# Seven-product multiplication kept for the second MLP matrix only, with weight sums moved from GpSimd to accumulating transfers and VectorE

## The reference

```python
    hf = rmsnorm(x, g_pre_ff)
    ff = jnp.einsum('btf,fd->btd', jnp.square(jax.nn.relu(jnp.einsum('btd,df->btf', hf, w_ff1) + b_ff1)), w_ff2) + b_ff2
    x = x + rmsnorm(ff, g_post_ff)
```

## Time and profile before

| what | us |
|---|---|
| median of 3 runs | 1292.96 (1291.39 to 1293.85) |
| time of the profiled execution | 1292.42 |
| its span, first to last instruction | 1290.9 |
| TensorE busy | 1203.9 |
| VectorE busy | 938.9 |
| ScalarE busy | 578.5 |
| GpSimd busy | 335.7 |

### The profile page before, as it was taken

The page is one execution under the profiler, slowest core; times in us unless marked ns, Lnnn a source line. Parts: engine busy times, 40 slices in busy tenths (PEclk is TensorE's granted clock), DMA queues, the critical chain, the costliest instruction groups (busy, mean ns, idle before and its releaser), DMA issues.

```text
span 1290.9 us, 23168 instructions
## 1 busy us (share of the span) xinstructions
PE 1203.9 (93%) x8749; PEld 1130.1 (88%) x8749; DVE 938.9 (73%) x1287; ACT 578.5 (45%) x914; POOL 335.7 (26%) x303
## 2 busy tenths in 40 slices
PE   9999999999999999999999999992898798799784
PEld 9999888978978888899999999992898798799783
DVE  6833888888888888874554333476778888888886
ACT  6433533543453453355432223564555544544543
POOL 4010011001101101100000000067557656656642
PEclk9999999999999999999999999995999899899888
DMA  6352244516516525422222234231232233232221
GB/s 215 108 178 100 66 160 169 170 57 226 182 43 233 189 65 175 152 94 87 87 92 83 80 97 151 83 152 35 64 115 67 75 93 95 66 98 83 66 103 69
DMA packets 47755, 145.97 MB, mean 113 GB/s; under 512 B 4756, under 2 KB 7188, under 8 KB 47304
## 3 DMA queue, kind: packets, MB, share of 16 engines
q1 hardware_dynamic: 36120, 103.74, 25.2%
q0 software_dynamic: 11424, 41.23, 9.1%
q10 hardware_dynamic: 144, 0.09, 0.0%
HBM read 120.54 MB, written 24.49 MB: 112 GB/s over the span
## 4 chain that ended last, share of the span: by engine, by line
PE 79%; DVE 12%; POOL 3%; issue 3%; ACT 3%; DMA 0%; DVEq 0%; ACTq 0%; POOLq 0%
PE product L2094 63%; PE side L2094 16%; POOL xg L746 1%; DVE cq L1977 1%; DVE wlo L1935 1%; ACT cq L1192 1%; DVE hlo L1912 1%; DVE wlo L1924 1%; DVE wlo L1930 1%; DVE hlo L1906 1%; DVE hlo L1904 1%; ACT whi L1217 0%; DVE yc L1847 0%; DVE wlo L1929 0%; DVE y L1842 0%
## 5 line engine op out<-in xcount | busy, mean ns | idle before, releaser
L2094 PE MATMUL product<-ahi,whi 128*128 128x272 f32 x1080 | 239.0, 295 | 25.7 <-DVE cq L1898 24.4
L2094 PE MATMUL product<-alo,whi 128*128 128x272 f32 x1080 | 233.7, 290 | 0.0
L2094 PE MATMUL product<-ahi,wlo 128*128 128x272 f32 x1080 | 233.3, 290 | 0.0
L1360 DVE TENSOR_TENSOR wlo<-wraw,whi 128x1024 fp32r<-128x1024 f32 x120 | 147.7, 1235 | 115.6 <-ACT whi L817 103.7
L817 ACT ACTIVATE whi<-wraw 128x1024 fp32r<-128x1024 f32 x120 | 125.9, 1054 | 199.1 <-PE product L2094 121.8
L2094 PEld LDWEIGHTS product<-ahi,whi 128*128 128x128 f32 x1080 | 175.5, 191 | 36.8 <-issue 35.9
L2094 PEld LDWEIGHTS product<-alo,whi 128*128 128x128 f32 x1080 | 175.4, 191 | 0.0
L2094 PEld LDWEIGHTS product<-ahi,wlo 128*128 128x128 f32 x1080 | 174.5, 191 | 0.0
L1573 DVE SCALAR_TENSOR_TENSOR accp<-u,wdw,accp 128x512 f32<-128x512 f32 x240 | 163.6, 743 | 0.7 <-DVE accp L1573 0.7
L702 POOL DMA_DIRECT2D out_c_s<-crg x32 | 17.1, 536 | 331.8 <-DVE crg L1695 325.1
L746 POOL TENSOR_SCALAR xg<-yc,col 128x544 f32<-128x544 f32 x8 | 17.2, 2172 | 305.5 <-DVE yc L1847 305.5
(11 more groups left out here) (400 smaller groups left out, 3153.0 us busy)
## 6 DMA issues: line engine op xcount, KB each, us to landing
wraw<-in_wstream SPq DMA_DIRECT2D x176, 512.0 KB, 3.7
crg<-in_c_in POOLq DMA_DIRECT2D x32, 512.0 KB, 6.8
out_c_s<-crg POOLq DMA_DIRECT2D x32, 512.0 KB, 3.2
hb<-head_rows POOLq DMA_DIRECT2D x4, 580.0 KB, 5.4
x<-in_xT SPq DMA_DIRECT2D x4, 544.0 KB, 6.5
sgm<-in_xT SPq DMA_DIRECT2D x1, 2176.0 KB, 9.2
x_rows<-yc SPq DMA_DIRECT2D x1, 2176.0 KB, 10.5
x1b<-x_rows SPq DMA_DIRECT2D x1, 2176.0 KB, 9.9
```

The source lines that it names most:

```text
L1360: V.tensor_tensor(wlo[:, k % RING, :, :], wraw[:, k % 2, :, :], whi[:, k % RING, :, :].bitcast(f32), ALU.subtract).then_inc(lo_done, 1)
L2094: return pe.matmul(out, lhsT, rhs, start=start, stop=stop, skip_group_check=check)
```

## The change

PLAIN becomes 10 (the first group's forms and one hidden tile pair more come from plain products). The other 11 pairs of w_ff1 tiles are "whole" units: two plain products T0 and T1 of 48 matmuls each, drained by one operation each (`evict`) with the token scale. Only the 16 down units use the seven products. Units are in a written order (ORDER_FF) that puts ups between downs.

The scheme of a down unit uses sums where the old one had differences: a11 is added into the loaded a21 by an accumulating transfer from DRAM, and a22 into a loaded a21 in its own buffer s1 in the same way. GpSimd issues both and does no arithmetic any more. VectorE makes s2 and s4 (`sums_made`), and the cross forms `tt` (`forms_made`). There are six form buffers and two more over the operand of w_ff1 for the last two pairs. xg, xtf, xthi, xtlo and rst_x are gone. The final residual is added by VectorE alone. SP's queue loads chunks 6 and 7, then unit 0 (whose s1 waits for the product of chunk 7), then chunks 8 and 9.

```diff
-PLAIN = 8
+PLAIN = 10
+C_UNITS = C_FF + PLAIN
+GROUPS, IN_GROUP, SLOTS = 4, 4, 6
+ORDER_FF = ("d0 u5 d0 d0 u6 d0 u7 u8 d1 u9 d1 d1 u10 d1 u11 u12 d2 u13 d2 u14 u15 d2 d2 d3 d3 d3 d3").split()
@@ sync
+            def unit_load(t):
...
+                if t == 0:
+                    sp.wait_ge(rows_used, 2)
+                elif t == 1:
+                    sp.wait_ge(lo_done, C_UNITS)
+                else:
+                    sp.wait_ge(split_lo, SPLIT_AT[t - 2, "first"])
+                    if is_down(t - 2):
+                        sp.wait_ge(sum_made, SUMS * order_of(t - 2) + SUMS - 1)
...
+                if is_down(t):
+                    d = order_of(t)
+                    if d < 2:
+                        sp.wait_ge(chunk_done, C_FF + KT)
+                    else:
+                        sp.wait_ge(split_lo, SPLIT_AT[DOWNS[d - 2], "sums"])
+                    sp.dma_start(s1[d % 2][:, :, :], wstream[two, :, 0:KT // 2, :]).then_inc(s1_in[d % 2], 16)
...
+            load_plain(6)
+            load_plain(7)
+            unit_load(0)
+            for k in range(8, PLAIN):
                 load_plain(k)
@@ gpsimd
-            (xg, xtf, cross_forms, weight_sums, the final additions)
+            for d, t in enumerate(DOWNS):
+                one, two = chunks_of(t)
+                pool.wait_ge(first_in[t % 2], first_due(t))
+                pool.dma_start(raw_of(t)[:, 0, KT // 2:KT, :], wstream[one, :, 0:KT // 2, :], accum_op=ALU.add).then_inc(s3_in[d % 2], 16)
+                pool.wait_ge(s1_in[d % 2], 16 * (d // 2 + 1))
+                pool.dma_start(s1[d % 2][:, :, :], wstream[two, :, KT // 2:KT, :], accum_op=ALU.add).then_inc(s1_sum[d % 2], 16)
@@ scalar, before the units
+            squared(0)
             hi(0, 4, C_FF + 6)
+            positive(1, 0)
+            positive(1, 1)
             squared(1)
             forms_plain(0)
+            hi(0, 4, C_FF + 7)
             forms_cross(0)
+            positive(2, 0)
+            positive(2, 1)
+            squared(2)
             forms_plain(1)
+            hi(0, 4, C_FF + 8)
             forms_cross(1)
...
@@ vector
+            def forms_made(p):
+                V.tensor_tensor(tt[:, 0:4:2, :], q[:, 0:4:3, :], q[:, 1:2, :].broadcast_to([P, 2, HALF]), ALU.subtract)
+                V.tensor_tensor(tt[:, 1, :], q[:, 3, :], tt[:, 0, :], ALU.add)
+                V.tensor_tensor(tt[:, 3, :], tt[:, 1, :], q[:, 2, :], ALU.subtract)
                 (then the three low splits, as before)
+            def sums_made(t):
+                V.tensor_tensor(s2[:, :, :], sum_1, a11, ALU.add).then_inc(sum_made, 1)
+                V.tensor_tensor(s4[:, :, :], a12, s2[:, :, :], ALU.add).then_inc(sum_made, 1)
+            def evict(t, m):
+                read(V.tensor_tensor(cq[:, p % 2, m:m + 1, :], across(banks(t)[m]).rearrange("p (a t) -> p a t", a=1), rst3,
+                                     ALU.mult), t, f"T{m}")
...
             plain_scaled(1, 1)
             lo(0, 4, C_FF + 6)
-            (two copies of rst, the forms of p = 0, xtlo)
+            forms_made(0)
             cq_free(0)
             plain_scaled(2, 0)
             lo(0, 4, C_FF + 7)
             plain_scaled(2, 1)
+            forms_made(1)
+            lo(0, 4, C_FF + 8)
             cq_free(1)
             plain_scaled(3, 0)
+            forms_made(2)
+            lo(0, 4, C_FF + 9)
             plain_scaled(3, 1)
+            sums_made(0)
             second_low(0)
+            forms_made(3)
+            first_low(0)
+            cq_free(2)
+            plain_scaled(4, 0)
+            (each unit t: the last read of t - 1, second_low(t), last_low(t), P1, sums_made(t + 1), P7, forms and T0 of an up,
+             first_low(t + 1), P6, P5, sums_low(t + 1), forms in a down, P2, P4)
@@ tensor
+            def whole(t, m):
+                pe.wait_ge(split_lo, SPLIT_AT[t, SPLIT_OF[f"T{m}"]])
+                bank_free(t, f"T{m}")
+                for kt in range(KT):
+                    for i, (a, b) in enumerate(((whi, ahi), (whi, alo), (wlo, ahi))):
+                        for g in range(2):
+                            ins = mm(piece(banks(t)[m], g), a[:, 2 * m, kt, :], b[:, kt, slice(*PARTS[g])],
+                                     kt == 0 and i == 0, kt == KT - 1 and i == 2)
```

More of the change, by code:

```diff
@@ L83 @@
[L83 to L90, removed]
+SPLIT_OF = {"P1": "first", "P7": "first", "P6": "sums", "P5": "sums", "P2": "second", "P4": "second", "P3": "last",
+            "T0": "first", "T1": "second"}
@@ new lines, in is_down, with steps_of, reader @@
+def is_down(t):
+    return UNITS[t][0] == "down"
+def steps_of(t):
+    return ("T0", "T1") if not is_down(t) else LAST if t == N_UNITS - 1 else MAIN
+def reader(t, name):
+    return "act" if UNITS[t][0:2] == ("down", 0) and name not in ("P6", "P5") else "dve"
+DONE, READ_AT, LAST_USE, SPLIT_AT = {}, {}, {}, {}
+_reads, _used, _splits = {"act": 0, "dve": 0}, {}, 0
+for _t in range(N_UNITS):
+    for _name in steps_of(_t):
+        DONE[_t, _name] = len(DONE) + 1
+        _reads[reader(_t, _name)] += 1
+        READ_AT[_t, _name] = _reads[reader(_t, _name)]
+        for _p in PLACE[_name]:
+            LAST_USE[_t, _p] = _used.get(_p)
+            _used[_p] = (_t, _name)
+    for _name in (("second", "first", "sums", "last") if _t == 0 else ("first", "sums", "second", "last") if is_down(_t)
+                  else ("first", "second")):
+        _splits += 1
+        SPLIT_AT[_t, _name] = _splits
@@ L742, in _ @@
             pool.dma_start(n_p, npn[:, :, :]).then_inc(small_saved, 16)
[L744 to L747, removed]
-            pool.wait_ge(xg_ready, KT)
-            near, far = xg[:, 0:KT // 2, :], xg[:, KT // 2:KT, :]
-            pool.tensor_tensor(xtf[:, 0, :, :], near[:, :, HALF:TT], near[:, :, 0:HALF], ALU.subtract).then_inc(xt_made, 1)
@@ new lines, in _ @@
+            first_low(0)
+            cq_free(2)
+            plain_scaled(4, 0)
+            for t in range(N_UNITS):
+                kind, g, n = UNITS[t]
+                more, end = kind == "down" and g > 0, t == N_UNITS - 1
+                if t == 0:
+                    cq_free(3)
+                    plain_scaled(IN_GROUP, 1)
+                    sums_low(0)
+                elif not is_down(t - 1):
+                    evict(t - 1, 1)
+                elif UNITS[t - 1][1] > 0:
+                    n_ = UNITS[t - 1][2]
+                    add_to(corners(yacc[:, 2 * n_:2 * n_ + 2, :])[:, 1, :], t - 1, "P3")
+                    if UNITS[t - 1][1] == GROUPS - 1:
+                        was_read(dve, t - 1, "P3")
+                        add_common(n_).then_inc(y_whole, 1)
+                if t > 0:
+                    second_low(t)
+                if kind == "down":
+                    last_low(t)
+                    y4, e = corners(yacc[:, 2 * n:2 * n + 2, :]), common[:, n, :]
@@ L2057, in _ @@
+                if not end and is_down(t + 1):
+                    sums_low(t + 1)
+                if kind == "down":
+                    for p in FORMS_IN[t]:
+                        forms_made(p)
+                if more:
+                    add_to(y4[:, 0, :], t, "P2")
+                    add_to(y4[:, 2, :], t, "P4", ALU.subtract)
+            t = N_UNITS - 1
             dve.wait_ge(y_squared, 2)
             V.tensor_tensor(cq[:, 0, :, :], cq[:, 0, :, :], cq[:, 1, :, :], ALU.add).then_inc(y_summed, 1)
-            was_read(dve, s, "P6")
@@ L2060, in _ @@
[L2060 to L2065 removed]
+            was_read(dve, t, "P6")
+            was_read(dve, t, "P7")
@@ L2502, in _ @@
+            for t in range(N_UNITS):
+                for name in steps_of(t):
+                    if is_down(t):
+                        seventh(t, name)
+                    else:
+                        whole(t, int(name[1]))
+                    if t == N_UNITS - 1 and name == "P5":
                         pe.wait_ge(y_summed, 3)
[L2503 to L2505 removed]
```

713 lines of the change are left out of this document (288 added, 425 removed).

## The result

The changed kernel took 1237.51 us (median of 4, 1237.26 to 1239.08), the kernel before 1292.85 beside it (median of 4): a ratio of 0.9575, 95% interval 0.9559 to 0.9592, 55 us less. The profiled execution took 1237.45 us with a span of 1235.9; the forecast was 1243.0 of span and 1245 of time.

What follows compares the result with a forecast made beforehand. TensorE, busy 93%, was taken as the bound, with 96 us lost after 872 us. Start 915.1 + 1.0, units 299.5 + 3.5 + 4, last pair 4.3, end 17.25 - 1.7: span 1243.0, time 1245, range 1236 to 1256 (chance 0.58).

Steps and rivals of the forecast that it cites:

- rival 1: All flows: the 4 and 3.5 us don't appear, loads land early; 1234 us or a little less, chance 0.13.
- the first wait: Plain start, before chunk 6: TensorE stops at 872 and waits 3.1 us instead of 24.4, until 875.1.
- The dip: Plain start, after the 11.6 us wait before chunk 8: the clock falls as after the old wait, 2.8 us charged.
- the overfull units: Pairs 14 and 15, two downs in a row that also make forms: backlog into the last group's first unit, 3.5 us.
- small waits: In the units: 4 us more, since four downs at 937 to 972 ran without a wait.
- unit 0's sums: At unit 0's start: 1.0 us added for its sums split, which needs chunk 9's slot.
- The end: After the last pair, 17.25 us: final additions by VectorE alone, two of 1.28 instead of one of 3.45, 1.7 us less.
- The bubbles of the up pairs (L2025) go with the pairs: Up units: the eight waits for over_hi, 29.1 us, vanish because a whole product is read once at its end.
- Rival 2: VectorE's fixed order stays late: up to 1 us at 20 of 27 unit starts; 20 us, 1265, chance 0.19.
- Rivals 3 and 4: Accumulating transfers: rival 3, near 20 us, 1269, chance 0.06; rival 4, much longer, slower than before, chance 0.04.
- My bound of 10.8 us of cover: Runs of downs: an accumulating transfer into s1 costs nothing if it lands within 10.8 us.
- My 32 issues of 528 to 536 ns: Trace evidence cited against the skill's rule that VectorE operations in a two-port mode keep GpSimd from writing descriptors.

Runs made afterwards that it cites:

- The early loads: The changed kernel with SP's queue loading chunks 8 and 9 before unit 0's weights: 1229.11 us, ratio 0.951 to the kernel before.
- The later hold: The changed kernel with the accumulating transfer into s1 held until unit t - 1's third product (first in a whole unit): 1315.48 us, ratio 1.0183.
- The runs with memsets: Memsets for GpSimd's sums and cross forms in the kernel before: short 1242.26 us, longer 1248.82; 16 memsets beside each of eleven down units, changed kernel: 1237.68.

## Why the prediction was right, and where it was not

**The forecast** of 1245 was 7.5 us too high; the result lies 1.5 us inside the low end of its range, nearer to rival 1 than to the forecast.

**The work of TensorE** was right: whole units take 12.0 us, down units 10.48 to 10.50.

**The start** was right step by step: the first wait ended at 874.25 for 875.1, chunk 8 began at 898.4 for 898.7, unit 0 at 914.4 for 915.1. The dip cost about 2.3 us, half of 898.4 to 903; I had charged 2.8:

```profile
893.00:898.40 5.40, 0.00 (x0) 0.00 (x0) 3.08 (x4) 2.06 (x2) 0.00 (x0) 0.50 0.36 84
898.00:903.00 5.00, 4.47 (x20) 4.50 (x21) 3.87 (x7) 3.56 (x5) 0.00 (x0) 0.52 0.00 0
```

The early loads show that the wait was what I took it for.

**The units** were mis-sized: 3.5 us for the overfull units, 4 for small waits and 1.0 for unit 0's sums are 8.5, and 3.8 were lost. That is 4.7 of the 7.1 us of the span's error. The overfull units and the one behind them lost 2.1 (252 matmuls from 1152.62 to 1186.18, 33.6 us for 31.5), most of it in the last group's first unit, where the prediction had put the backlog.

**The end** was the other term: 1.7 us forecast, 3.3 measured. VectorE's part is 9.7 us instead of 11.9. I left out that each half of the rows is now sent as soon as it is done, so that after VectorE's last addition 3.8 us pass instead of 5.0. That and rounding make the sum.

**Where the gain came from** was told wrongly, though the time was right. The step that failed is "The bubbles of the up pairs (L2025) go with the pairs". Three quarters of them go when GpSimd stops reading, with all 28 seven-product pairs in place: 29.1 us fell to 7.5. The slowing, which I counted as 28 x 0.6 us of VectorE's time at L1935, was the cause of some 44. It lay in the chain of an up pair, where additions, scaling, ReLU, forms and splits follow one another, so that each slow VectorE step came back as a TensorE wait and then as half clock. The plain ups bought little by themselves as far as these runs show: four of them take 48.0 us, four seven-product pairs beside memsets 46.0, and what else the change saved in the units (18.5 us) is what its added matmuls cost (18.0). The total came out near all the same, because the sum was built from the new kernel's steps and no term of it hung on how the old loss divides. Whether seven-product ups would be faster with VectorE making their sums as well wasn't tried, so it stays open.

**Rivals.** Rival 1 (all flows) said 1234 or a little less, 3.5 us below the result; it was nearer in the units, not in the start. Rival 2 did not appear. Rivals 3 and 4 were not met, the transfers landing in 4.1 and 6.1 us by the median for the 8 that I took, but one took 11.4, above the 11 that I had named as a sign. Their mechanism is real: landing 14.5 us later than now, the kernel is slower than before. My bound of 10.8 us of cover was fair: landing 8.8 us later than the present 6.1 costs 3.7 us. The price beyond it is steeper than I worked out. The later hold is like a landing time of some 20.6 us (6.1 + 14.5, an estimate), for which I had 24 us, and it cost 78; I had let only the downs in a run pay, and every down does. My 32 issues of 528 to 536 ns were no test of what a copy on VectorE does to an issue: beside them VectorE ran operations with two SBUF inputs and never an fp32 copy, and no run here shows it.

## What to carry to other kernels

Ask of a helper engine not only how long its work takes but what its reads do to the engine that works beside it: replacing its operations with writes of the same outputs is a cheap test of that. A queue position is part of a step's cost: two loads and one pair of sums moved within their queues gave 13.9 us with no work removed. A sum that comes out near the measured time doesn't show that its account of the gain is right; only an experiment on the kernel before did that here. When a wait vanishes, look at once for what stood second in the same queue.

## What the runs showed of the hardware

VectorE's operation with two SBUF inputs (128x1024) takes 1.22 us alone or beside GpSimd memsets, and up to 2.67 beside a GpSimd tensor_tensor; one with an input from PSUM stays at 0.43 us in all of these kernels. The Trainium skill, "SBUF — State Buffer", section "Who interferes with whom", says just this: a VectorE instruction with two SBUF inputs contends with a GpSimd instruction that reads SBUF, not with one that only writes. The runs with memsets bear it out; what they add is the size, 44 us of 1293.

An accumulating transfer of 256 KB took 4.1 or 6.1 us to land (medians), a plain one of the same size from SP 3.9; its issue held GpSimd for 0.86 to 1.04 us against 0.53 for a plain transfer of 512 KB.

The granted clock was 0.50 from 893 to 898.4 us, in the later part of the wait of 12 us, and 0.52 from 898 to 903, after matmuls had begun again. It stayed at 1.00 from 914.4 to 1222 us, where no wait of TensorE was longer than 1.3 us.
